# Larger pieces of the first latent head, its first maxima taken inside the window attention, and sixteen repeated products at the end of the input projections

## The reference

```
xn  = rmsnorm(x) ;  h = xn @ w_in          # split: c_q | c_kv | k_rope | window q, k, v
q   = rmsnorm(c_q) @ w_uq (+ rope)         # 8 latent heads, 64 + 32 wide
k,v = rmsnorm(c_kv) @ w_ukv                # same heads, 64 wide each
A   = softmax(mask(q k^T) * scale) v       # latent attention, block-causal in chunks of 64
B   = softmax(q k^T * scale + bias, sink) v  # window attention, 8 heads, window 128
x   = x + rmsnorm(concat(A, B) @ w_out)
x   = x + rmsnorm(conv_ffn(rmsnorm(x)))    # gated MLP with a causal convolution of width 3
```

## Time and profile before

| | us |
|---|---|
| median of 3 runs | 2572.74 (2569.98 to 2573.74) |
| the profiled execution's own time | 2566.74 |
| its span, first to last instruction | 2564.9 |
| PE busy | 2481.0 (97% of the span) |
| DVE busy | 2051.7 (80%) |
| ACT busy | 1310.3 (51%) |
| mean granted TensorE clock | 0.985 |

### The profile page before, as it was taken

The page is one execution under the profiler, slowest core; times in us unless marked ns, Lnnn a source line. Parts: engine busy times, 40 slices in busy tenths (PEclk is TensorE's granted clock), DMA queues, the critical chain, the costliest instruction groups (busy, mean ns, idle before and its releaser), DMA issues.

```text
span 2564.9 us, 43834 instructions
## 1 busy us (share of the span) xinstructions
PE 2481.0 (97%) x15855; PEld 2297.4 (90%) x15855; DVE 2051.7 (80%) x2854; ACT 1310.3 (51%) x2434; POOL 627.8 (24%) x503
## 2 busy tenths in 40 slices
PE   8999979899999999999999999899999999999997
PEld 7999965577777779998999999899999999999997
DVE  6877767788878874979899888788888778796976
ACT  5444338567666775435444443444444455545453
POOL 1111031233434443541110000044444000311212
PEclk9999989899999999999999999999999999999999
DMA  7666656545444434354633333654444267777754
GB/s 214 231 224 224 214 180 172 125 79 87 87 83 79 86 94 159 136 203 163 244 124 118 116 108 118 242 155 144 147 148 150 92 232 255 249 269 273 274 192 155
DMA packets 280439, 425.98 MB, mean 166 GB/s; under 512 B 61348, under 2 KB 216836, under 8 KB 278404
## 3 DMA queue, kind: packets, MB, share of 16 engines
q1 hardware_dynamic: 280228, 423.25, 53.1%
HBM read 305.10 MB, written 118.84 MB: 165 GB/s over the span
## 4 chain that ended last, share of the span: by engine, by line
PE 44%; DVE 4%; DMA 2%; issue 2%; ACT 0%; POOL 0%; SPq 0%; DVEq 0%; ACTq 0%
PE mf_ps L2659 30%; PE mf_ps L2699 14%; DMA mf_area<-h_scr 1%; DMA mix_rest<-h_scr 1%; DVE mf_area L3238 0%; DVE mf_area L3291 0%; DMA mf_area<-xn_scr 0%; DMA h_scr<-mf_area 0%; DVE mix_rest_rounded L3266 0%; DVE mix_rest L3291 0%; DVE mf_area L3241 0%; POOL mf_area L2560 0%; DVE mf_area L3316 0%; ACT mf_area L2894 0%; DVE mix_rest_rounded L3275 0%
## 5 line engine op out<-in xcount | busy, mean ns | idle before, releaser
L2659 PE MATMUL mf_ps<-mf_rounded,mix_rest_rounded 128*128 128x264 f32 x4752 | 676.1, 285 | 7.5 <-DVE mf_area L3190 4.6
L2659 PEld LDWEIGHTS mf_ps<-mf_rounded,mix_rest_rounded 128*128 128x128 f32 x4752 | 620.3, 189 | 8.8 <-DVE mf_area L3190 5.3
L2699 PE MATMUL mf_ps<-mf_rounded,mf_rounded 128*128 128x352 f32 x1914 | 416.6, 324 | 5.4 <-DVE mix_rest_rounded L3275 2.8
L2699 PEld LDWEIGHTS mf_ps<-mf_rounded,mf_rounded 128*128 128x128 f32 x1914 | 325.7, 188 | 8.1 <-issue 3.1
L2659 PE MATMUL mf_ps<-mf_rounded,mf_rounded 128*128 128x264 f32 x1584 | 280.4, 285 | 7.2 <-DVE room_rounded L3142 6.6
L1665 PE MATMUL at_ps<-ahead_q,ahead_k 96*128 96x512 f32 (+8 forms) x1008 | 258.2, 365 | 0.4 <-DMA ahead_q<-la_turned_top 0.4
L1722 ACT ACTIVATE la_prob<-at_ps 128x512 f32<-128x512 f32 (+1 forms) x336 | 175.5, 522 | 153.8 <-PE at_ps L1665 140.4
L1765 DVE TENSOR_REDUCE la_part<-at_ps 128x1 f32<-128x512 f32 (+4 forms) x328 | 188.9, 595 | 60.3 <-PE at_ps L1651 58.0
L2659 PEld LDWEIGHTS mf_ps<-mf_rounded,mf_rounded 128*128 128x128 f32 x1584 | 229.0, 189 | 8.0 <-issue 6.2
L1665 PEld LDWEIGHTS at_ps<-ahead_q,ahead_k 96*128 96x128 f32 (+2 forms) x1008 | 180.2, 192 | 37.8 <-DMA ahead_q<-la_turned_top 0.6
L1466 POOL TENSOR_TENSOR la_low<-la_prob,la_high 128x512 fp32r<-128x512 f32 (+3 forms) x109 | 123.7, 1134 | 272.0 <-ACT la_high L1723 244.9
(11 more groups left out here) (291 smaller groups left out, 5373.3 us busy)
## 6 DMA issues: line engine op xcount, KB each, us to landing
mix_rest<-in_w_up SPq DMA_DIRECT2D x168, 256.0 KB, 2.9
pi_w_raw<-in_w_in SPq DMA_DIRECT2D x49, 512.0 KB, 6.2
mf_area<-h_scr SPq DMA_DIRECT2D x12, 1936.0 KB, 10.3
mix_rest<-h_scr SPq DMA_DIRECT2D x9, 1936.0 KB, 9.4
mf_area<-sums_scr SPq DMA_DIRECT2D x24, 704.0 KB, 4.1
mf_area<-in_w_down SPq DMA_DIRECT2D x18, 704.0 KB, 4.6
h_scr<-mf_area SPq DMA_DIRECT2D x22, 528.0 KB, 4.1
mf_area<-in_w_down SPq DMA_DIRECT2D x128, 88.0 KB, 2.1
```

Of the source, the lines that this page charges most:

```text
L2659: mm = pe.matmul(pair[slots[i]][:, e], w[:, k], x[:, e * HB:(e + 1) * HB], start=(k == 0 and m == 0 and i < 5), stop=(k == KH - 1 and m == 2),
L2699: mm = pe.matmul(out, l[:, w], r[:, x], start=(k == 0 and e == 0 and i in (0, 1, 5)), stop=(k == HALF - 1 and e == 2), skip_group_check=True)
```

## The change

In the input projections, PE appends sixteen products of 128x128 by 128x424 after its last expansion. They read operands still in place and write a bank of `acc` that nobody reads any more; the wait before them is for a count reached long ago. In the window attention, SP's turns are put in another order with larger pieces: queries and keys of the first latent head in quarters (turns 2, 4, 6, 8 and turns 9 to 12), values in pairs of tiles (turns 1 to 8, the rest in turn 13); `keep(t-2)` moves up to stand behind `load_qk`, and `spread(t-2)`, one tile earlier than before, stands last. `between` is called twice in each step; at steps 15, 16 and 17 it takes five groups of two chunks (`EARLY`): all four of the first unit, the one of the second unit, and five of the eight of the third. The rows of the first two units are sent from SP's window part. POOL's splitting of the first values moves one tile later.

```
+            pe.wait_ge(acc_free, TILES - 1)
+            for again in range(16):
+                pe.matmul(acc[:, (TILES - 2) % 2, 0:TB], wx_hi[:, 16], x_hi[:, (BLOCKS - 2) % 2, 0, 0:TB], start=True, stop=True)
...
-            cols = slice(i * (TOK // 8), (i + 1) * (TOK // 8))        # queries; keys alike with KEYS // 8
+            cols = slice(i * (TOK // 4), (i + 1) * (TOK // 4))
...
         for t in range(NT + 1):
             if t + 3 <= NT:
                 load_qk(t + 3)
+            if t >= 2:
+                keep(t - 2)
             if 2 <= t + 1 <= NT:
                 load_v(t + 1)
-            if t >= 3:
-                spread(sp, t - 3)
-            if t >= 4:
-                store(sp, t - 4)
-            if 2 <= t < 10:
-                head_values(2 * t - 4)
-                head_values(2 * t - 3)
-            if t == 10:
+            if 1 <= t < 9:
+                head_values(t - 1)
+            if t in (2, 4, 6, 8):
+                head_queries(t // 2 - 1)
+            if 9 <= t < 13:
+                head_keys(t - 9)
+            if t == 13:
...
-            if t < NT:
-                if t % 2:
-                    head_keys(t // 2)
-                else:
-                    head_queries(t // 2)
+            if t >= 4:
+                store(sp, t - 4)
+            if t == NT:
+                first_row(0)
             if t >= 2:
-                keep(t - 2)
-        spread(sp, NT - 2)
-        store(sp, NT - 3)
-        first_row()
-        keep(NT - 1)
+                spread(sp, t - 2)
+        keep(NT - 1)
+        first_row(1)
+        store(sp, NT - 3)
         spread(sp, NT - 1)
+        keep(NT)
         store(sp, NT - 2)
-        keep(NT)
...
-    VALUES_AT = 12
+    VALUES_AT = 13
...
-            if t == NT:
-                between(pe)
+            between(pe, 2 * (t - NT + 1))
             if t <= NT:
                 turn_v(t)
                 turn_first(t)
+            between(pe, 2 * (t - NT + 1) + 1)
...
+    EARLY = {0: ((0, 0), (0, 1)), 1: ((0, 2), (0, 3)), 2: ((1, 0), (2, 0)), 3: ((2, 1), (2, 2)), 4: ((2, 3), (2, 4))}
+    EARLY_OF_2 = 5
+
-    FIRST_SPANS = {1: (0, 0), 2: (0, 2), 3: (3, 9), 4: (10, 20)}
+    FIRST_SPANS = {2: (0, 2), 3: (3, 9), 4: (10, 20)}
...
-                pe.wait_ge(ahead["in"], 16 * 5 * 8)
+                pe.wait_ge(ahead["in"], 16 * 5 * 4)
```

More of the change, by code:

```diff
@@ L1228, in vector @@
                 front(t + 2)
-            if t == NT:
-                between(dve)
+            between(dve, 2 * (t - NT + 1))
+            between(dve, 2 * (t - NT + 1) + 1)
             if t > 0:
@@ L1344, in plan @@
             for pos, span in FIRST_SPANS.items():
-                out += [(i, p, pos, m) for m in due(s, span, len(max_chunks(ORDER[pos])))]
+                early = EARLY_OF_2 if pos == 2 else 0
+                out += [(i, p, pos, early + m) for m in due(s, span, len(max_chunks(ORDER[pos])) - early)]
         for pos in range(len(ORDER)):
@@ L1591, in tail @@
                 sp.wait_ge(moved[a], 80 * PLACES.count(a) * HEADS // 2)
-        return (lambda: row(0, 0, 0)), (lambda: walk(sp, step, tail))
+        return (lambda pos: row(0, 0, pos)), (lambda: walk(sp, step, tail))
     def fills(pool):
@@ L1605, in first_values @@
     def first_values(pool, m):
-        pool.wait_ge(ahead["v_in"], 16 * V_TILES)
+        pool.wait_ge(ahead["v_in"], 16 * V_LATE)
         hi, lo = v_piece(0, m)
@@ L1687, in value_tile, with early @@
                       skip_group_check=True).then_inc(pv_done, 1)
-        def prologue():
-            pe.wait_ge(wa["rows_set"], wa["rows_count"])
-            pe.wait_ge(wa["biased"], 4 * wa["tiles"] + 4)
-            for m in range(len(max_chunks(ORDER[0]))):
-                max_chunk(0, 0, 0, m)
+        def early(k):
+            if k == 0:
+                pe.wait_ge(wa["rows_set"], wa["rows_count"])
+                pe.wait_ge(wa["biased"], 4 * wa["tiles"] + 4)
+            for pos, m in EARLY.get(k, ()):
+                max_chunk(0, 0, pos, m)
         def step(i, p, s, more):
@@ L1705, in tail @@
                 value_tile(LAST, 1, s)
-        if begin:
-            prologue()
+        if begin is not None:
+            early(begin)
         else:
@@ L1739, in step @@
                 if m == 0:
-                    act.wait_ge(ahead["v_in"], 16 * (V_TILES + V_LATE * (2 * j + g)))
+                    act.wait_ge(ahead["v_in"], 16 * V_LATE * (2 * j + g + 1))
                 hi, lo = v_piece(g, m)
@@ L1792, in maxima_after, with early @@
                 maxima(i, p, pos)
-        def prologue():
-            dve.wait_ge(wa["rows_set"], wa["rows_count"])
-            for m in range(len(max_chunks(ORDER[0]))):
-                maxima_after(0, 0, 0, m)
+        def early(k):
+            if k == 0:
+                dve.wait_ge(wa["rows_set"], wa["rows_count"])
+            for pos, m in EARLY.get(k, ()):
+                maxima_after(0, 0, pos, m)
         def step(i, p, s, more):
@@ L1853, in tensor @@
     def tensor(pe):
-        wa["tensor"](pe, lambda eng: la["tensor"](eng, True))
-        la["tensor"](pe, False)
+        wa["tensor"](pe, la["tensor"])
+        la["tensor"](pe, None)
     def scalar(act):
@@ L1861, in vector @@
     def vector(dve):
-        wa["vector"](dve, lambda eng: la["vector"](eng, True))
-        la["vector"](dve, False)
+        wa["vector"](dve, la["vector"])
+        la["vector"](dve, None)
     return {"sync": sync, "gpsimd": gpsimd, "tensor": tensor, "scalar": scalar, "vector": vector}
```

9 lines of the change are left out of this document (5 added, 4 removed).

## The result

The changed kernel takes 2557.62 us as a median of 4 runs (2553.49 to 2559.32), the kernel before 2573.24 in runs beside it. The ratio is 0.9943, 95% interval 0.9929 to 0.9956: between 11 and 18 us faster. Timed once more, with 15 runs of the kernel before beside it, it was 0.9947 (0.9934 to 0.9961), 10 to 17 us. The forecast was 11.9 us and 2560.8.

What follows compares the result with a forecast made beforehand. PE bounds the kernel, but SP's queue paces tiles 8 to 15 and the join is slow. Terms -6.8 - 2.35 - 1.7 + 1.1 - 2.16 = -11.9 take the median 2572.74 to 2560.8 us; 8-in-10 range 2554 to 2571.

Steps and rivals of the forecast that it cites:

- Part 1: Window attention, tiles 8 to 15: fewer issues stop SP pacing, removing PE's waits for rec_rows, -6.8 us.
- price by issue: SP's queue: a piece of twice the bytes issues in about the same time, some 17 us saved.
- Part 2: Join: PE's wait for the latent head's last key piece goes, -2.35 us.
- At nothing: Join, steps 15 to 17: six more chunks of maxima on DVE, 0.575 us each, cost no time.
- Part 3: Latent attention's opening: POOL's scaling and split decide; terms -1.7, +1.1, -2.16 us; PE stands 3 to 5 us.
- -2.16 us: First value product: the gap between the end of POOL's split and PE's product, counted as gained.
- Part 4: Block's end: sixteen products end near 355 at no cost and gain 0; ends -1.0 and +1.6 us.
- The sum: Whole kernel: all terms together -11.9 us, profiled execution 2554.8, median 2560.8 us.
- SP stays the pacemaker: Rival, window attention: byte-priced issues or SP's waits eat the saving, only 3.4 us at the join left, 2569.3; chance 0.16.
- closing loop: Rival, SP's turn: keep, spread and the next loads wait on each other, +6.8 us, 2579.5; chance 0.09.
- slow opening: Rival, latent attention: PE stands longer, then runs at half clock, -8.3 us in all, 2564.4; chance 0.14.
- after a stand, about the same: 0: Latent attention after the first value product: clock loss unchanged, 0; ends -2 and +3.6 us.

Runs made afterwards that it cites:

- d: Changed kernel with the old, smaller piece sizes, two in each place, same bytes in the same turns, 28 issues more; 2569.85 us, ratio 0.9993 to the kernel before.
- e: Kernel before with only the larger pieces, in the changed kernel's turns; old SP order, old join, no repeats; 2566.69 us, ratio 0.9976 to the kernel before.
- f: Changed kernel with the old join: only the first unit's chunks early, in step 16, its row sent alone; 2559.76 us, ratio 0.9945 to the kernel before.
- c: Changed kernel with POOL's splits of the first values one tile earlier, where they were before; 2560.67 us, ratio 0.9946 to the kernel before.
- j: Changed kernel with value splits a tile earlier, spread(15) ahead of SP's store and cached values loaded in SP's second turn; 2557.31 us, ratio 0.9948 to the kernel before.
- h: Changed kernel with value splits a tile earlier and spread(15) ahead of SP's store; 2559.53 us, ratio 0.9944 to the kernel before.
- a: Changed kernel without the sixteen repeated products; 2560.08 us, ratio 0.9951 to the kernel before.

## Why the prediction was right, point by point

**Part 1, SP's turns: the size right, the reason half of it.** The term was -6.8 us for tiles 8 to 15, and the traces show 48.89 - 42.07 = 6.8. The price by issue held, as the queue's rows show (0.56 us for a piece of double size) and as d proves at equal bytes. Wrong was the length of the new turns: 6.3 us were forecast for one with keys, "at or within 0.1 us" of the tile, and they took 7.0, the quickest two 6.5. SP didn't cease to be the slower one there; it was ahead by enough. What I had also not seen is that fewer issues alone don't give the gain. Beside each other, d (all of the change but the sizes) is at 0.9993, e (the sizes alone) at 0.9976 and both together at 0.9943 to 0.9947. The two alone would make 0.9993 x 0.9976 = 0.9969; the other 0.0024, 6 us, comes only with both. By the intervals of the three ratios it is uncertain to some 0.0018; the marks are plainer: at `turn_v(15)` d is 5.4 us behind the kernel before, e 0.6 ahead of it, and both together 6.5 to 7.9 ahead. The prediction spoke of the move of `keep` as free of danger, and gave it no share in the gain. f against e says that the order is worth 0.0031, 8 us, once the sizes are there. No run moves `keep` or `spread` alone, so that it is the distance between the two is read from the traces: between `keep(t-2)` and `spread(t-2)` now lie 3.6 us of other issues in a turn with keys (433.43 to 437.00, the store's end), and SP's waits for landings of the reciprocals, 10.6 us in e, are 0.5 us from 356 to 500 in the changed kernel.

**Part 2, the keys: right.** -2.35 was forecast; from `turn_v(15)` to `(16)` it is 5.82 us and not 8.59, that is -2.8. With e at 6.07 this comes from the turn in which the last piece is loaded. DVE carried the early chunks there, 4.39 us busy of 5.82, and PE waited 0.3 us for it. "At nothing" holds for this step and not for the next, as part 3 shows.

**Part 3, what is late next: the chain right, two terms wrong, and its worth not shown.** I said that PE would stand 3 to 5 us before its first value product, waiting for POOL. It stands 3.03 us, and starts 0.1 us after POOL's split ends at 484.18 (the profile writes "issue" for it; in the six traces with such a stand, d's among them, the product starts 0.1 us after the split's end, and in c, with the split a tile earlier, there is none):

```profile
481.41 1.26 POOL L1029 TENSOR_TENSOR wa_outT<-wa_outT,wa_rec_all 128x512 f32<-128x512 f32 x1 [4.30 <-issue]
...
483.19 0.99 POOL L1618 TENSOR_TENSOR ahead_v<-ahead_v 128x384 fp32r<-128x384 f32 x1
```

`scale(15)` was forecast for 479.0; with the 2.56 us by which this execution was late from the start that is 481.6, and it came at 481.41; the product, forecast behind 481.8, came at 484.28 - 2.56 = 481.7. But two errors cancel here, and that is luck. The chain took 481.41 - 468.37 = 13.0 us and not 11.7 (12.6 in the second trace). In the kernel before, the two halves of the third row are:

```profile
467.91:476.50 8.59, 5.70 (x31) 3.31 (x31) 3.38 (x10) 5.87 (x22) 2.70 (x3) 0.94 0.39 111
476.50:485.05 8.55, 7.57 (x37) 2.95 (x35) 5.10 (x13) 3.68 (x13) 3.69 (x4) 0.66 0.41 114
```

So the clock behind `turn_v(16)` rose from 0.66 to 0.81 only, and the stretch to the first score tile became longer, 8.90 us for 8.55. Less the 1.1 us for the row and the store, the chain gained 0.3 us on its 12.28 (0.7 in the second trace) and not the 1.7 of the forecast. In f and e, with the old join and the clock at 1.00 there, it takes 9.9 and 9.6 us, so more than 1.7 could be had. And the chunks taken early, costed at nothing, may not be free on this chain: j has them at a clock of 1.00, and its chain takes 10.3 us though `spread(15)` no longer stands behind a store of 1.4. How much of the 3 us between f and the changed kernel is the chunks and how much the clock, no run separates.

The other error: `turn_v(16)` was 1.5 us earlier than forecast. 1.1 of it lie ahead of tile 8 (66.98 us from the last expansion to `turn_v(8)`, against 68.08 before) and 0.4 between `turn_v(15)` and `turn_v(16)`. In the second trace the opening took 68.54 us, `turn_v(16)` came at 116.42, where the forecast had 116.41, and the first value product at 131.94, 1.1 later than forecast.

Of the -2.16 us the trace has the mark, but c, f, h and j say that the mark isn't time. Moving that product by up to 4 us, or taking the stand away, left the ratio between 0.9944 and 0.9948. (2.16 us alone are 0.0008, less than these ratios resolve; it is the four together, and their marks, that speak.) From `turn_v(16)` to the 17th product the changed kernel takes 45.2 and 47.8 us against 47.3 before. So the gain that can be shown is 10.7 and 9.1 us at `turn_v(16)`, where 6.8 + 2.35 = 9.15 had been forecast; of the 2.76 us that part 3 put behind it, the one trace shows 2.1 and the other none.

**Part 4, the repeats: right in the two traces.** End near 355 forecast; 357.8 less the 2.56 is 355.2, and 356.1 in the second. No gain, and no cost that the time shows, though h and j lose 0.9 us of marks to them. The Trainium skill ("TensorE: Matmul & The Clock Gate", Part 1: The HAM clock gate) holds that sustained activity releases the full rate. The rows agree: the first sixteen scores took 2.08 us before and 1.16 now. It is the time that didn't follow, because a full clock ahead of a wait for a transfer buys a longer wait: DVE's bias add came 12.29 us after the last expansion before, 11.89 in a, and 12.12 and 12.43 in the two traces with the repeats. DVE's wait for the cached values in front of it was 1.78 us before and 1.42 in a, and 3.60 and 3.38 with them.

**The sum.** -11.9 us on the profiled execution would be 2554.8; it was 2557.44. The difference is the 2.56 us lost ahead of the change. The second trace doesn't fit as well: 2559.74, of which 1.25 were lost ahead of the change, so that 3.7 us are missing, 3.2 of them already at the 17th product. Against the runs the forecast was 2560.8, and they gave 2557.62 and 2559.68. The interval of the ratio holds -11.9 us both times. Whether the true gain is 12 or 14 us these runs don't tell; if it is 14, the 2 to 3 us beyond the steps have no place in a trace that I could name.

**The rivals.** That SP stays the pacemaker is refuted by PE's steps and the time, not by SP's waits: SP stayed as full, at 7.0 us a turn with keys, and it was spared by its head start, which these turns brought down from 8.1 to 3.5 us. The closing loop, slower, didn't come: with key turns of the changed kernel the steps stay at 6.25. It did come in part in e, where `spread` stands directly behind `keep`. The slow opening is there in one of the two traces. In the 16.2 us after the stand the clock is 0.79 in the first, better than the 0.72 of the earlier trace rows, and 0.61 in the second. The two products behind the first one after the stand took 0.39 and 0.40 us in the first trace and 0.63 each in the second, so only the second ran them at the lower level; at the 17th product the leads over the kernel before are 12.8 and 8.7 us, where the forecast had 11.9 and that rival 8.3. So these two aren't rivals but two ends of what one program does, and the term "after a stand, about the same: 0" should have carried both.

## What to carry to other kernels

When one queue paces a stage, count its issues and, separately, the distance in that queue between a store and the load that reads it back: fewer issues only help if the queue doesn't then stand for the landing, and here the sizes alone were worth 6 us, the rest alone nothing clear of the noise, and both 14. A queue that is slower than the stage for a few turns does no harm as long as its head start lasts, so look at that too, and read its waits by stage. A wait on the critical chain that is followed by a stretch of half clock and by other waits of like length is no reserve: taking it away moved marks by up to 4 us and the time by nothing that could be told. Before reading a difference of 2 to 3 us out of two traces, set both to a mark ahead of the first changed instruction, and look at a second trace of the same kernel.

## What the runs showed of the hardware that was not expected

The granted clock at the join differs between executions of the same program by as much as all the join's edits. From `turn_v(16)` to the 17th product, with the same instructions, the changed kernel's two traces give:

```profile
468.37:513.59 45.22, 38.78 (x178) 27.13 (x176) 34.70 (x75) 21.60 (x58) 12.37 (x13) 0.89 0.56 103
```

```profile
468.61:516.37 47.76, 42.02 (x178) 29.86 (x177) 35.75 (x75) 21.61 (x58) 12.18 (x13) 0.79 0.53 98
```

and j, with 1.7 us less of PE's idle time (4.7 against 6.4) than the first of these, lies between:

```profile
468.76:514.46 45.70, 40.99 (x178) 29.40 (x176) 34.47 (x75) 21.59 (x58) 10.83 (x11) 0.81 0.57 102
```

Idle time saved there came back as busy time at the lower level. It isn't the rule: in f and e, with the old join, PE is idle for 4.6 and 4.4 us of this stage, at a clock of 0.85 and 0.88, and the stage takes 44.9 and 43.5 us. What decides which clock an execution gets there, these traces don't show.
